# Hybrid decoder layer on one core: reads ahead of casts, the samples' A by one product, and another order in the last pass

## What is computed

```python
h = rmsnorm(x, g_pre_mix)
proj = h @ w_in                      # q|k|v, beta, decay, z, GLU input, gate a, gate b
qkv = silu(causal_dwconv(qkv_pre, 4 taps));  q, k = l2norm(q), l2norm(k)
# branch A, per head and block of tokens:
a = where(strict, beta * (k @ k.T) * decay, 0)
sol = triangular_solve(a + I, [beta * v, beta * exp(gam) * k])
u = vw - kd @ s;  o = qd @ s + qk @ u;  s = gl * s + ko.T @ u
o_a = rmsnorm(o) * silu(z)
# branch B:
c = causal_dwconv(glu[:, :C] * sigmoid(glu[:, C:]), 31 taps) + bias
o_b = silu(layernorm(c))
mixed = sigmoid(gate_a) * o_a + sigmoid(gate_b) * o_b
x = x + rmsnorm(mixed @ w_out, g_post_mix)
y = x + rmsnorm(relu(rmsnorm(x, g_pre_ffn) @ w_up) ** 2 @ w_down, g_post_ffn)
```

## Time and profile before

| | us |
|---|---|
| median of three runs | 1165.0 (1164.53 to 1168.1) |
| the profiled execution, its own time | 1162.98 |
| its span | 1161.0 |
| TensorE busy | 1116.0 |
| VectorE, ScalarE, GpSimd busy | 742.6, 523.8, 580.5 |

### The profile page before, as it was taken

One profiled execution on the slowest core, in us unless ns is written; L12 is line 12 of the kernel. 1 busy time (PEld: TensorE's weight loads), 2 busy tenths in 40 slices (PEclk: granted clock), 3 DMA queues, 4 the chain that ended last, 5 costly groups with the idle time before them and its releaser, 6 DMA issues.

```text
span 1161.0 us, 23218 instructions
## 1 busy us (share of the span) xinstructions
PE 1116.0 (96%) x8791; PEld 1064.2 (92%) x8791; DVE 742.6 (64%) x1178; ACT 523.8 (45%) x939; POOL 580.5 (50%) x512
## 2 busy tenths in 40 slices
PE   6799999999999999999999989999999999999996
PEld 5588989999899999998998879999999999999996
DVE  6669897897978979799775266763145115314735
ACT  6554545545555455554564576432133123214431
POOL 0328548475583755838565363234343434335831
PEclk9799999999999999999999999999999999999998
DMA  6121222212221122311222115122323222323302
GB/s 235 45 77 38 84 77 90 72 36 83 76 96 63 36 85 74 101 58 36 85 93 73 55 48 201 55 74 73 89 75 91 73 90 73 90 74 90 108 22 82
DMA packets 32521, 92.12 MB, mean 79 GB/s; under 512 B 4688, under 2 KB 12240, under 8 KB 32464
## 3 DMA queue, kind: packets, MB, share of 16 engines
q1 hardware_dynamic: 32464, 91.32, 24.9%
HBM read 82.79 MB, written 8.52 MB: 79 GB/s over the span
## 4 chain that ended last, share of the span: by engine, by line
PE 78%; DVE 9%; ACT 7%; issue 6%; DMA 0%; POOL 0%; DVEq 0%; ACTq 0%; SPq 0%
PE ps L577 29%; PE ps L606 26%; PE ps L615 6%; PE ps L945 4%; DVE ps L1408 3%; DVE work L1405 2%; PE ps L831 1%; PE ps L746 1%; PE ps L765 1%; ACT w_hi L1025 1%; PE ps L625 1%; PE ps L777 1%; DVE o_a L1408 1%; PE ps L638 1%; DVE conf L1405 1%
## 5 line engine op out<-in xcount | busy, mean ns | idle before, releaser
L1900 POOL TENSOR_TENSOR w_lo<-raw,w_hi 128x1024 fp32r<-128x1024 f32 x123 | 298.5, 2427 | 388.7 <-ACT w_hi L1043 225.8
L606 PE MATMUL ps<-in_hi,w_hi 128*128 128x288 f32 x992 | 306.3, 309 | 5.9 <-ACT work L1121 3.1
L606 PE MATMUL ps<-in_hi,w_lo 128*128 128x288 f32 x992 | 302.5, 305 | 0.0
L606 PE MATMUL ps<-in_lo,w_hi 128*128 128x288 f32 x992 | 299.1, 302 | 0.0
L606 PEld LDWEIGHTS ps<-in_hi,w_hi 128*128 128x128 f32 x992 | 189.1, 191 | 10.3 <-ACT work L1124 4.2
L606 PEld LDWEIGHTS ps<-in_hi,w_lo 128*128 128x128 f32 x992 | 189.0, 191 | 3.3
L606 PEld LDWEIGHTS ps<-in_lo,w_hi 128*128 128x128 f32 x992 | 188.9, 190 | 1.1
L1408 DVE SCALAR_TENSOR_TENSOR ps<-work,ct,ps 128x512 f32<-128x512 f32 x240 | 180.7, 753 | 7.4 <-DVE work L1531 1.7
L1043 ACT CAST w_hi<-raw 128x1024 fp32r<-128x1024 f32 x61 | 63.8, 1047 | 224.3 <-PE ps L577 224.3
L1405 DVE TENSOR_TENSOR f_tmp<-f_tmp 128x576 f32<-128x576 f32 x31 | 70.8, 2285 | 96.3 <-ACT f_tmp L1355 91.0
L1405 DVE TENSOR_TENSOR o_a<-o_a,ps 128x576 f32<-128x576 f32 (+1 forms) x40 | 25.3, 634 | 144.7 <-PE ps L577 122.8
(11 more groups left out here) (308 smaller groups left out, 2271.1 us busy)
## 6 DMA issues: line engine op xcount, KB each, us to landing
raw<-w_all_in SPq DMA_DIRECT2D x136, 512.0 KB, 3.6
work<-s_in_in SPq DMA_DIRECT2D x8, 512.0 KB, 3.4
s_sample_out<-work SPq DMA_DIRECT2D x8, 512.0 KB, 2.7
xt<-x_t_in SPq DMA_DIRECT2D x4, 576.0 KB, 6.5
xt<-x_t_in SPq DMA_DIRECT2D x2, 1152.0 KB, 7.1
y_out<-o_a SPq DMA_DIRECT2D x16, 144.0 KB, 1.7
halo<-halos_in SPq DMA_DIRECT2D x9, 156.0 KB, 3.5
conf_rows_out<-c_rows SPq DMA_DIRECT2D x8, 135.0 KB, 2.1
```

The costliest lines, as they stand in the source:

```text
L606: t = mm(dense_ps(n, j, h), a[:, w, k], b[:, k, h * HALF:(h + 1) * HALF], start=r == 0, stop=r == PASS_MM // 2 - 1)
L1900: return gp.tensor_tensor(out, a, b, op)
```

## The change

It has five parts.
1. `casts` is a function of its own. In passes 1 to 8 ScalarE reads a slot's halves first and casts then; pass 0 keeps casts first.
2. The samples' `db` (64x64) is not made any more. The samples' A is `dm` by beta by the product in PSUM in one instruction.
3. GpSimd makes the first U in slot 5, directly behind the first masks; it was in slot 6, behind that slot's casts and product.
4. Last pass, convolution: VectorE sums the samples in slots 3 and 6 (5 and 8 before); the last nine taps are spread as 3, 2, 2, 2 over slots 1, 2, 6 and 8 (over 1, 2, 3, 6 before).
5. Last pass, slots 24 to 31: W_out's casts and splits 0 to 2 are in slots 24, 28 and 30 (24, 25, 26). ScalarE's copies of chunk 3 and of the samples come ahead of the second four Silus; the copy of chunk 4 comes in slot 28 ahead of both reads of job 7. GpSimd multiplies blocks by their gate one slot sooner. VectorE adds no block in slot 28 and four in slot 29.

The core of the diff:

```diff
--- before.py
+++ after.py
...
                 out.append((n, 6))
             if last(n) and s == 1:
                 out.append((n, 2))
-            if last(n) and s in (24, 25, 26):
-                out.append((8, ("out", s - 24)))
+            if last(n) and s in (24, 28, 30):
+                out.append((8, ("out", (24, 28, 30).index(s))))
             return out
...
                           ACT.Copy).then_inc(act_read, 1)
+            def casts(n, s):
+                for m, off in splits(n, s):
+                    if isinstance(off, tuple):
+                        split(8, off[1])
+                    else:
+                        proj_split(m, off)
+
+            def chunk_u(n, c):
+                act.wait_ge(u_ps, TILES * n - 3 + c)
+                A(tile(v["u"], c), g(1)[:, 0:P], ACT.Copy,
+                  scale=hc[:, 5 * BETA + c:5 * BETA + c + 1]).then_inc(u_ready, 1)
+
+            def samples_u(n):
+                act.wait_ge(us_ps, n)
+                A(smw(v["u"]), g(1)[0:SMP, P:2 * P], ACT.Copy,
+                  scale=hc[0:SMP, 5 * BETA + 4:5 * BETA + 5]).then_inc(us_ready, 1)
+
             def phase(n):
                 gdn = not first(n)
                 for s in range(33):
-                    for m, off in splits(n, s):
-                        if isinstance(off, tuple):
-                            split(8, off[1])
-                        else:
-                            proj_split(m, off)
+                    if first(n):
+                        casts(n, s)
+                    if last(n) and s == 28:
+                        chunk_u(n, 3)
+                        for h in range(2):
+                            act.wait_ge(job_done, 2 * (base(n) + 7) + 1 + h)
+                            half_read(n, 7, GB, h)
                     pos, j = evac_first(n, s)
-                    if pos is not None:
+                    if pos is not None and not (last(n) and pos == 7):
                         act.wait_ge(job_done, 2 * (base(n) + pos) + 1)
                         if j == GA:
...
                         half_read(n, pos, j, 0)
                     pos, j = evac(n, s)
-                    if pos is not None and not (first(n) and j == CB) and not (last(n) and pos == 9):
+                    if pos is not None and not (first(n) and j == CB) and not (last(n) and pos in (7, 9)):
                         act.wait_ge(job_done, 2 * (base(n) + pos) + 2)
                         half_read(n, pos, j, 1)
+                    if not first(n):
+                        casts(n, s)
                     if not last(n) and s in conv_slots(n, 2)[not first(n):]:
...
                         act.wait_ge(sz_ps, n)
                         A(v["cs0"], g(2)[:, 0:SMP], ACT.Copy).then_inc(sz_ready, 1)
-                    if s in (22, 24, 26, 28):
-                        c = (s - 22) // 2
-                        act.wait_ge(u_ps, TILES * n - 3 + c)
-                        A(tile(v["u"], c), g(1)[:, 0:P], ACT.Copy,
-                          scale=hc[:, 5 * BETA + c:5 * BETA + c + 1]).then_inc(u_ready, 1)
+                    if s in (22, 24, 26) or s == 28 and not last(n):
+                        chunk_u(n, (s - 22) // 2)
+                    if s == 26:
+                        samples_u(n)
                     if last(n) and s in (24, 26):
...
                             A(conf[:, k], conf[:, k], ACT.Silu, scale=pcol("ln_g", k),
                               bias=pcol("ln_b", k)).then_inc(b_silu, 1)
-                    if s == 26:
-                        act.wait_ge(us_ps, n)
-                        A(smw(v["u"]), g(1)[0:SMP, P:2 * P], ACT.Copy,
-                          scale=hc[0:SMP, 5 * BETA + 4:5 * BETA + 5]).then_inc(us_ready, 1)
                     if s == 28:
                         act.wait_ge(os_ps, n)
...
                 if s == 4:
                     dve.wait_ge(dm_ready, n)
-                    tt(pr(v["db"]), pr(v["dm"]), hcol(BETA), ALU.mult)
-                    tt(sm(v["db"]), sm(v["dm"]), hcol_s(BETA, SMP), ALU.mult).then_inc(db_ready, 1)
+                    tt(pr(v["db"]), pr(v["dm"]), hcol(BETA), ALU.mult).then_inc(db_ready, 1)
                 if s == 5:
                     dve.wait_ge(kk_ps, n)
...
                     for i in range(2):
                         tt(quad(v["at"], i, 0), quad(g(0), i, i), quad(v["db"], i, i), ALU.mult)
-                    tt(sm(v["at"]), g(2)[0:SMP, 0:SMP], sm(v["db"]), ALU.mult).then_inc(at_ready, 1)
+                    stt(sm(v["at"]), sm(v["dm"]), hc[0:SMP, 5 * BETA + 4:5 * BETA + 5], g(2)[0:SMP, 0:SMP],
+                        ALU.mult, ALU.mult).then_inc(at_ready, 1)
                     dve.wait_ge(hm_ready, n)
...
             early = {1: 3, 2: 1, 3: 3, 8: 2}
-            early_8 = {1: 3, 2: 2, 3: 2, 6: 2}
+            early_8 = {1: 3, 2: 2, 6: 2, 8: 2}
             late = {22: 2, 23: 2, 24: 4, 25: 2, 26: 2, 27: 2, 28: 2, 29: 2, 30: 2, 31: 2}
             late_1 = {24: 4, 25: 2, 26: 3, 27: 2, 28: 3, 29: 4, 30: 2, 31: 2}
...
                     t = CF_TAPS - sum(rest.values()) + sum(rest[x] for x in rest if x < s)
                     conf_taps(n - 1, t, t + rest[s])
-                samples = (5, 8) if last(n) else (14, 18)
+                samples = (3, 6) if last(n) else (14, 18)
                 if gdn and s in samples:
                     conf_samples(n - 1, samples.index(s))
...
                     if last(n) and 28 <= s < 32:
-                        for k in {28: (0, 1), 29: (2, 3, 4), 30: (5,), 31: (6,)}[s]:
+                        for k in {28: (), 29: (0, 1, 2, 3), 30: (4, 5), 31: (6,)}[s]:
                             dve.wait_ge(b_gated, k + 1)
                             tt(conf[:, k], conf[:, k], o_a[:, k], ALU.add).then_inc(mixed, 1)
...
                         tt(pr2(c_r[0]), both(v["at"]), lvl(1), ALU.mult)
                         tt(c_s[0][0:SMP], sm(v["at"]), lvl_s(1), ALU.mult).then_inc(c1_ready, 1)
-                    if s == 6:
-
                         pool.wait_ge(c1_ready, n)
                         tt(pr2(uc_r), ident2(), pr2(c_r[0].bitcast(F32)), ALU.subtract)
                         tt(v["us"][0:SMP], con("ident", SMP)[:, 0:SMP], c_s[0][0:SMP], ALU.subtract).then_inc(u0_ready, 1)
+                    if s == 6:
                         pool.wait_ge(qk_ps, n)
                         tt(v["qn"], v["qn"], v["eg"], ALU.mult).then_inc(qd_ready, 1)
...
                            v["eg"][:, SEQ + LS - 1:TOK:LS].unsqueeze(2).to_broadcast([P, NS, P]),
                            ALU.mult).then_inc(ss_decayed, 1)
-                    if last(n) and s in (25, 26, 27, 28, 30):
-
-                        for k in {25: (0, 1, 2), 26: (3,), 27: (4,), 28: (5,), 30: (6,)}[s]:
+                    if last(n) and s in (24, 25, 26, 27, 29):
+
+                        for k in {24: (0, 1, 2), 25: (3,), 26: (4,), 27: (5,), 29: (6,)}[s]:
                             gate_b(k)
                     if last(n) and s == 31:
...
```

## The result

The changed kernel takes **1154.3 us** (median of 5 runs, 1152.1 to 1157.4) against 1165.0 (5 runs): a ratio of 0.991, 95% interval 0.9886 to 0.9934. The two profiled executions, 1154.3 and 1163.0, lie 8.6 us apart.

What follows compares the result with a forecast made beforehand. TensorE, busy 96% of the span, could gain only from waits, half clock or earlier inputs; -2.6 - 1.7 - 2.8 + 1.5 = -5.6 us took 1163.0 to 1157.4, with 2.0 to the median 1159.4; range 1157.0 to 1164.8.

Steps and rivals of the forecast that it cites:

- so all go: **-2.6: Passes 1 to 7: with reads ahead of casts, TensorE's seven waits for ScalarE's read L1124 vanish, -2.6 us.
- the seven waits at L746 go: **-1.7: Passes 1 to 7: without the samples' separate product, T is ready 2.3 us earlier and the L746 waits vanish, -1.7 us.
- I take it that VectorE is first by 0.07 us: Passes 1 to 7: VectorE's tap copy starts at 451.89, GpSimd's w_lo at 451.96, so the copy is not held.
- the wait at L746 takes back what the reads gave: Passes 1 to 7, rival: GpSimd is first and the copy is held; +0.3 instead of -4.3, 1164.0 us, chance 0.20.
- The 2.2 us: Last pass, slots 4 to 9: TensorE's wait at L765 for GpSimd's start of U goes, 2.2 us.
- all of it starts some 6 us sooner: Last pass: GpSimd's work ahead of the next masks starts some 6 us sooner, TensorE only 2.2, so they are covered.
- The new wait: Last pass's end: job 9 needs block 7's bank, whose reads stand behind the fourth chunk's copy; TensorE waits 1.3 us.
- the wait at W_out: W_out's first matmul: TensorE, through with job 9 at 678.2, waits 4.4 us for the additions.
- -2.8 was put: Start of W_out: at 682.5 to 682.6 against 685.37, since the additions let only -2.8 of 6.6 us arrive.
- 6.6 had been summed: VectorE's last state update in the last pass: from 677.40 to 670.8, by -7.9 for waits and half clock, +1.3 for a new wait.
- +1.5 put: Clock at W_out's start: the 4.4 us wait likely brings the lower level, costing +1.5 us, between 0 and twice that.
- The median of the three runs lies 2.0 higher, at 1165.0; I forecast **1159.4: Whole kernel: 1157.4 us for the profiled execution plus the 2.0 offset of before's median; chance 0.50.

Runs made afterwards that it cites:

- E1: Kernel before with ScalarE reading its half blocks ahead of casts in every pass but the first: 1166.8 against 1163.2 us, ratio 1.0032.
- E2: Kernel before with only the samples' A made by one product that reads PSUM: 1162.8 against 1163.2 us, ratio 0.9995.
- E6: Kernel before with both reads ahead of casts and one product for the samples' A, last pass's convolution and end unchanged: 1162.4 against 1162.8 us.
- E7: Kernel before with only GpSimd's start of U moved to slot 5: 1162.5 against 1162.8 us, ratio 0.9995.
- E12: Kernel before with only VectorE's last-pass sample sums in slots 3 and 6, two taps in slot 8: 1160.6 against 1164.1 us, ratio 0.9971.
- E3: Kernel before with only the last pass's end changed, reads ahead of casts only there: 1163.0 against 1163.2 us, ratio 1.0005.
- E10: Changed kernel with U's start back in slot 6 and sample sums back in slots 5 and 8: 1160.0 us against 1162.9 for the kernel before.
- E4: Changed kernel with additions of blocks 0 to 4 in slot 28, block 5 in slot 29: 1151.0 us against 1163.2 for the kernel before.

## Why the prediction was off

The sign and each mechanism were right; the sum was too small by 3.1 us against the trace and by 5.1 against the medians.

**Passes 1 to 7: the term mis-sized.** The steps "so all go: **-2.6**" and "the seven waits at L746 go: **-1.7**" took the idle time that the list of waits shows as what the waits cost. In pass 6 that is 0.22 and 0.25. By start times each of passes 3 to 7 gives 0.79 to 0.81, of which in pass 6 0.48 at the read and 0.32 at L746; pass 2 gives 1.26 where 0.95 is listed. Start times in the timeline of before, where TensorE's matmuls follow each other by 0.13:

```profile
451.38 0.29 PE L606 MATMUL ps<-in_lo,w_hi 128*128 128x288 f32 x1
...
452.12 0.29 PE L606 MATMUL ps<-in_hi,w_lo 128*128 128x288 f32 x1
```

The one that waits stands between them at 451.88, so these two steps take 0.50 and 0.24, in all 0.48 more than twice 0.13. The listed idle time begins only where the record of the matmul ahead ends, 0.29 behind its start, though the next could have started after 0.13, and the matmul behind the waiting one comes late too. At L746 it is 459.33 to 459.86 before, 0.53, and 454.13 to 454.35 after, 0.22: 0.31 less. Over six passes this makes 5.3 where 3.3 was put: 2.0 of the 3.1 us.

**The hold.** "I take it that VectorE is first by 0.07 us" held, by 0.01: the sign of the largest term hung on a margin smaller than the error of its working, and that it came out right was luck. That all passes or none have it held as well (six of six in E1, E2, E6). The Trainium skill's page "SBUF — State Buffer" (SBUF: two separate sides) has the one that starts first keep the access for its whole instruction; the 166 ns of E6 and the 2335 ns of E1 agree. The price of the other case, worked out as "the wait at L746 takes back what the reads gave", is what E1 shows: 0.48 gained and 0.46 lost in pass 6, 0.1 us gained over passes 2 to 7 where +0.3 had been put.

**L765.** The 2.2 us were right (2.3). "all of it starts some 6 us sooner" was the part that counted, though it came to some 4: E7, without VectorE's earlier sum, meets the masks; E12 needs nothing else.

**The end of the last pass.** The new wait measured 1.25 (1.3 put), the time from the update to the last addition's end 10.9 (664.17 to 674.32 + 0.74; 11.2 put), the wait at W_out 4.0 (4.4). Together with L765 it is -3.5 where -2.8 was put: another 0.7. About 0.3 of it is the additions. Another 0.3 is the update, which came 6.9 us sooner within the last pass where 6.6 had been summed, and that is the same step as in the passes: by start times the waits at L819 and L798 cost 2.0 and 3.1 us (1.7 and 2.5 listed), and the new one of 1.25 costs 1.5.

**The clock.** +1.1 against +1.5 put is two things, and their sum is near by luck. At the lower level W_out's first matmuls lose some 2.3 us by their start times. But before had a second wait at W_out, 998 ns long at 687.80, which costs 1.2 us there and is gone, and of which the prediction said nothing:

```profile
PE ps L615 <- DVE in_lo L1405: 1.5, 2, 1.0
```

What was missed besides is that the clock is a cost of L765 as well. The prediction said of the wait of 2.2 that it did not bring the lower level. That was one execution. The same wait costs 1.5 us more in E1 and E3, 2.9 in E10 and 4.3 in E6. The forecast compares two executions of which neither has this loss. But of what E6's kernel gains from the passes, nothing arrives until the wait at L765 is gone as well (0.5 us of 5.3 in E6); the term of 2.2 stood for more than itself.

**From the profile to the median.** "The median of the three runs lies 2.0 higher, at 1165.0; I forecast **1159.4**" carried the offset of before's profiled execution over to the changed kernel. The changed kernel's profiled execution is its median. The first stage took from 143.4 to 146.5 us in the fourteen traces. The two ends are E10 and E4, whose programs are the same up to there, so this is no effect of the change, and the draw lies in every single time. With it, the 8.6 us between the profiled executions became 10.7 in one set of runs and 8.0 in the other. Whether the clock's fall behind L765 lies in some of the unprofiled runs of before isn't shown: in the two traces that have before's order there (before, E2) it doesn't.

## What to carry to other kernels

Price a wait of TensorE by the start times around it (here 0.5 us for 0.22 listed), not by the idle time listed. Where a short VectorE instruction is held by a GpSimd one, removing it hands the hold to the next in line; look at what starts behind it, and whether another part of the change moves the GpSimd instruction. Parts of such a change can't be judged one by one: reads, product and end change the time by +3.5, -0.4 and -0.2 us alone (the last two no more than noise), and the first two are worth 5.3 together as soon as no wait behind them gives it back.

## What the runs showed of the hardware

A VectorE instruction that started 9 to 10 ns ahead of GpSimd's w_lo (pass 6 of E1 and of the changed kernel) ran in its own time (0.21 and 0.16 us), and one that started 0.13 to 0.34 behind it (E1, E2) took 2.34 and 2.35 us, to w_lo's end. A wait of 2.2 us of TensorE at the same place was followed by full clock in before and E2, and by 1.2 GHz for about 3.4 us (E3; 1.5 lost in E1 as well), 7 (E10) and 10 (E6). The 250 matmuls ahead of it (4500 to 4750) take 34.2 us in all six. The four in which the clock fell have the reads ahead of the casts in the last pass, the two in which it stayed have not; how ScalarE's order could do that isn't shown, and with one trace each it may be chance.
